# Reordering the loads that open each layer of a two-layer decoder step

## What is computed

```python
z = x @ w_in            # 1024 -> conv gates, q, six k/v parts, attention gates, two merge gates
u = ua * sigmoid(ug)                              # branch A: causal depthwise conv (31 taps),
conv_out = silu(layer_norm(conv(u_ext))) @ w_conv_out     # LayerNorm, swish, projection
pkc, pvc, pks, pvs = gather_pages(cache, page_table)      # branch B: paged past K/V of the samples
k_cmp = compress(kc_all, cmp_pe_k, cmp_w1_k, cmp_w2_k)    # blocks of 32 rows -> one row
o_cmp, p_cmp = cmp_attention(q, k_cmp, v_cmp, q_pos)
o_slc = slc_attention(q_rot, ks_all, vs_all, q_pos, select_blocks(p_cmp, q_pos, n))
o_win = win_attention(q_rot, kw, vw)
m = sigmoid(g_a) * conv_out + sigmoid(g_b) * (gated sum of the three @ w_attn_out)
x = layer_norm(ALPHA * x + m @ w_o)
x = layer_norm(ALPHA * x + (silu(x @ w_gate) * (x @ w_up)) @ w_down)
```

## Time and profile before

| | us |
|---|---|
| median of 3 runs | 1043.68 |
| lowest, highest | 1042.11, 1046.44 |
| the profiled execution, device time | 1041.28 |
| its span, first to last instruction | 1039.5 |
| PE busy in it | 979.4 (94%) |

### The profile page before, as it was taken

One profiled execution on the slowest core, in us unless ns is written; L12 is line 12 of the kernel. 1 busy time (PEld: TensorE's weight loads), 2 busy tenths in 40 slices (PEclk: granted clock), 3 DMA queues, 4 the chain that ended last, 5 costly groups with the idle time before them and its releaser, 6 DMA issues.

```text
span 1039.5 us, 23311 instructions
## 1 busy us (share of the span) xinstructions
PE 979.4 (94%) x7438; PEld 928.7 (89%) x7438; DVE 603.1 (58%) x1370; ACT 524.5 (50%) x966; POOL 753.9 (73%) x1081
## 2 busy tenths in 40 slices
PE   6999989989999999999979999889989999999996
PEld 6898878878989999999979978888889999999996
DVE  2969765476577555512447795745685765554125
ACT  3352574465566655533444436745555565555335
POOL 5877746434978888898848786544369788889985
PEclk9999999999999999999999999999999999999999
DMA  8875586621446654454256566675124344445542
GB/s 302 282 252 201 183 275 212 231 80 62 163 153 206 232 202 163 162 182 162 85 198 235 162 199 193 240 232 194 64 71 160 134 163 163 163 163 170 175 143 107
DMA packets 78917, 185.09 MB, mean 178 GB/s; under 512 B 9538, under 2 KB 42690, under 8 KB 78530
## 3 DMA queue, kind: packets, MB, share of 16 engines
q1 hardware_dynamic: 70290, 167.03, 47.9%
q10 hardware_dynamic: 8352, 15.59, 4.5%
q0 software_dynamic: 144, 0.89, 0.2%
HBM read 170.90 MB, written 12.57 MB: 177 GB/s over the span
## 4 chain that ended last, share of the span: by engine, by line
POOL 52%; issue 25%; PE 20%; DMA 1%; POOLq 1%; DVE 1%; ACT 1%; ACTq 0%; SPq 0%; DVEq 0%
POOL w_lo L620 46%; PE proj L691 4%; PE proj L693 4%; PE proj L692 4%; POOL hid L643 3%; POOL res L641 2%; PE proj L714 2%; PE proj L712 2%; PE proj L713 2%; DMA res<-xT_in 1%; POOLq L638 0%; POOLq L614 0%; POOL res L650 0%; DVE res L1572 0%; DVE sig_u L1639 0%
## 5 line engine op out<-in xcount | busy, mean ns | idle before, releaser
L620 POOL TENSOR_TENSOR w_lo<-wch,w_hi 128x256 fp32r<-128x256 f32 x940 | 686.4, 768 | 267.9 <-ACT w_hi L1100 267.5
L691 PE MATMUL proj<-x_hi,w_hi 128*128 128x290 f32 (+1 forms) x1248 | 381.6, 306 | 23.2 <-POOL w_lo L620 22.1
L693 PE MATMUL proj<-x_lo,w_hi 128*128 128x290 f32 (+1 forms) x1248 | 372.7, 299 | 0.0
L692 PE MATMUL proj<-x_hi,w_lo 128*128 128x290 f32 (+1 forms) x1248 | 371.7, 298 | 0.0
L1100 ACT ACTIVATE w_hi<-wch 128x1024 fp32r<-128x1024 f32 x235 | 247.7, 1055 | 155.5 <-PE proj L714 84.2
L691 PEld LDWEIGHTS proj<-x_hi,w_hi 128*128 128x128 f32 x1248 | 237.7, 190 | 30.3 <-POOL w_lo L620 13.7
L692 PEld LDWEIGHTS proj<-x_hi,w_lo 128*128 128x128 f32 x1248 | 238.1, 191 | 0.6
L693 PEld LDWEIGHTS proj<-x_lo,w_hi 128*128 128x128 f32 x1248 | 237.6, 190 | 0.0
L712 PE MATMUL proj<-hid_hi,w_hi 128*128 128x288 f32 x352 | 104.3, 296 | 0.0
L714 PE MATMUL proj<-hid_lo,w_hi 128*128 128x288 f32 x352 | 104.1, 296 | 0.0
L713 PE MATMUL proj<-hid_hi,w_lo 128*128 128x288 f32 x352 | 103.5, 294 | 0.0
(11 more groups left out here) (288 smaller groups left out, 1521.8 us busy)
## 6 DMA issues: line engine op xcount, KB each, us to landing
wch<-weights_in SPq DMA_DIRECT2D x235, 512.0 KB, 3.7
pg<-slc_pages_in SPq DMA_DIRECT2D x128, 128.0 KB, 2.3
pg<-cmp_pages_in SPq DMA_DIRECT2D x96, 128.0 KB, 2.9
wn<-win_in SPq DMA_DIRECT2D x16, 512.0 KB, 5.2
win_out<-wn ACTq DMA_DIRECT2D x4, 2048.0 KB, 9.1
pg<-cmp_pages_in ACTq DMA_DIRECT2D x32, 128.0 KB, 3.8
hid<-w_in SPq DMA_DIRECT2D x2, 1024.0 KB, 5.8
kv_out<-kv ACTq DMA_DIRECT2D x2, 864.0 KB, 3.5
```

Source lines behind the costliest of these rows:

```text
L620: last = nc.gpsimd.tensor_tensor(lo[:, cols], raw[:, cols], hi[:, cols].bitcast(F32), ALU.subtract)
L691: mm(ps, hi[:, kb], x[0][:, kb, 0:n], start=kb == 0, stop=False)
L692: mm(ps, lo[:, kb], x[0][:, kb, 0:n], start=False, stop=False)
L693: last = mm(ps, hi[:, kb], x[1][:, kb, 0:n], start=False, stop=kb == KD - 1)
```

## The change

Six edits:

1. The page table is fetched by ACT, as its first instruction, and no longer by SP.
2. In the first layer SP's wait for the table moves from ahead of chunk 3 to behind it. The pages of the lead move one chunk later in both layers (behind chunks 3 to 18, no longer 2 to 17).
3. In the second layer the wait for the end of the layer before and the load of `sm` move from behind chunk 2 to behind chunk 4.
4. `w1` and `w2` move from behind chunk 3 to behind chunk 8, in both layers.
5. GpSimd issues the constants after its first three subtractions, no longer as its first work.
6. `small_in` counts `sm` alone; a new counter `w1_in` counts `w1` and `w2`, and PE waits for it ahead of the first compression matmul.

```diff
-        small_in = Signal("small_in", 3, 16)
+        small_in = Signal("small_in", 1, 16)
+        w1_in = Signal("w1_in", 2, 16)
...
-                    if j == SLOTS - 1:
+                    if j == (SLOTS - 1 if first else SLOTS + 1):
                         wait_alone(*x_ready(layer, 0))
                         small_in.up(sp.dma_start(sm[:], small[bass.ds(layer, 1)].rearrange("a p n -> p (a n)")))
                         if first:
-                            sp.dma_start(table[:], page_table).then_inc(table_in, 16)
                             load_past(layer)
-                            sp.wait_ge(table_in, 16)
-                    if j == SLOTS:
-                        small_in.up(sp.dma_start(w1_sb, w1[bass.ds(layer, 1)].rearrange("a p b (c w) -> p (a b) c w", c=KD)))
-                        small_in.up(sp.dma_start(w2_sb[0:64], w2[bass.ds(layer, 1)].rearrange("a e c d -> e (a c) d")))
-                    if EARLY - 2 * PAGES <= j < EARLY:
-                        n = j - (EARLY - 2 * PAGES)
+                    if j == SLOTS and first:
+                        sp.wait_ge(table_in, 16)
+                    if j == 8:
+                        w1_in.up(sp.dma_start(w1_sb, w1[bass.ds(layer, 1)].rearrange("a p b (c w) -> p (a b) c w", c=KD)))
+                        w1_in.up(sp.dma_start(w2_sb[0:64], w2[bass.ds(layer, 1)].rearrange("a e c d -> e (a c) d")))
+                    n = j - (EARLY - 2 * PAGES) - 1
+                    if 0 <= n < 2 * PAGES:
...
-            pool.dma_start(cst[:], consts).then_inc(const_in, 16)
             pool.memset(u_p[:, :, 0:TAIL], 0.0)
...
             for n in range(PAIRS):
                 low_part(0, n)
+            pool.dma_start(cst[:], consts).then_inc(const_in, 16)
...
-                pool.wait_ge(*small_in(layer, 3))
+                pool.wait_ge(*small_in(layer, 1))
...
                 if c == 0 and sp_ == 0:
+                    pe.wait_ge(*w1_in(layer, 2))
                     pe.wait_ge(*xc_ready(layer, 1))
...
+            act.dma_start(table[:], page_table).then_inc(table_in, 16)
             now = {}
...
-                dve.wait_ge(*small_in(layer, 3))
+                dve.wait_ge(*small_in(layer, 1))
```

More of the change, by code:

```diff
@@ L473, in _ @@
         def _(sp):
-            for sig in chunk_in + [small_in]:
+            for sig in chunk_in + [small_in, w1_in]:
                 sig.begin(sp)
```

## The result

The changed kernel takes **1034.27 us**, median of 5 runs (1034.04 to 1037.84), against 1043.68 before. The ratio is 0.9917, 95% interval [0.9899, 0.9936]: about 9 us faster, 7 to 11 with the interval. The span of its profiled execution is 1032.4 us.

The account below looks back on a forecast made before the run. PE bounds the kernel (94% busy), so time could come only from its waits: four waits of 7.27 us, less 0.1 for ACT's new first instruction, take 7.2 off the median 1043.68, giving 1036.5 us, range 1033 to 1041.5.

Parts of the forecast that it names:

- The four waits: PE's waits ahead of chunks 3 and 4 in both layers close: 2.67 us in the first, 4.60 in the second.
- The span: Whole profiled execution: forecast to be 1034.1 us with a span of 1032.3, after 7.2 us off.
- the drops of the clock: PE at its lower clock after some idle stretches: 1.7 us each, booked as spread unrelated to the loads.
- ACT's new first instruction: Start of the first layer: ACT's issue of the table fetch delays rounding by 0.1 us, at worst 1.3.
- Chunk 3 at about 9: First layer: SP issues chunk 3 at about 9.0, 6.3 us earlier, with 2.0 us to spare; chunk 4 has 1.1.
- no stretch as empty as 13 to 15 us: Sign in the opening: the transfer engines' dry stretch, 44 GB/s between 13 and 15 us, does not stay empty.
- Chunk 5 behind the constants: First layer: constants issued in the same moment as chunk 5 cost nothing, at worst 1.2 us given back.
- Rival A: Constants and w1 displace chunks PE awaits (1.2, 0.8 us), or ACT's issue costs 1.3: 1038 to 1040, chance 0.20.
- Rival B: Table as late from ACT as before; chunk 5 then costs at most 1 us: 1037.5, chance 0.05.
- The new waits: SP's wait for the table, PE's for w1, VectorE's and GpSimd's for sm, and later pages: all cost nothing.
- no wait of PE for GpSimd between 521 and 590: Sign at the change of layers: PE never waits there for GpSimd in the trace after.
- The closed gaps: Sign against the forecast: they return as longer PE waits for VectorE and ACT between 90 and 300 us.

Follow-up runs that it names:

- e1: Kernel before with only the change of layers reordered as in the changed kernel, opening left as before, split counter kept: 1040.61 us, ratio 0.9959.
- e2: Kernel before with only the first layer's opening reordered as in the changed kernel, change of layers left as before, split counter kept: 1039.66 us, ratio 0.9956.
- before_again: The kernel before, unchanged, run and profiled a second time: 1044.69 us (one run).
- e5: Changed kernel with GpSimd issuing the constants as its first work again: 1035.29 us, ratio 0.9911.
- e8: Changed kernel with two more loads of the constants' size (1.74 MB) right behind the constants: 1037.57 us (one run).
- e7: Changed kernel with the page table fetched by SP as before, its wait staying behind chunk 3: 1035.42 us, ratio 0.991.
- e4: The changed kernel, unchanged, run and profiled a second time: 1036.2 us, ratio 0.9919.
- e3: Changed kernel with ACT issuing the page table's fetch behind its rounding of chunk 0: 1034.83 us, ratio 0.9915.
- e10: e9 with output 0 starting when a quarter of chunk 0 is ready and SP loading the constants behind chunk 10: 1033.97 us, ratio 0.9904.
- e6: Changed kernel with w1 and w2 early again, behind chunk 3 in layer 1 and behind chunk 4 and sm in layer 2: 1038.94 us, ratio 0.993.
- e9: Changed kernel with VectorE reading output 5 ahead of eight taps, and ACT fetching the table behind its rounding of chunk 0: 1035.62 us, ratio 0.9919.

## Why the prediction was right

The prediction was 1036.5 us, within 1033.0 to 1041.5, faster by over 0.5%. Measured: 1034.27. By its own steps:

- **The four waits, 7.27 us.** Right, in places and in mechanism: none is left, e1 and e2 bring back two each, and before_again has all four. The two leads shortened by 3.8 and 4.6 us, against 2.67 and 4.60 forecast.
- **The span, forecast as 1032.3 and measured as 1032.4.** That it agrees to 0.1 us is partly luck. The first lead gained 1.1 us more than forecast, the first matmul came 0.5 later and *rest* was 0.7 longer. The clock was also on the side of the trace before: 0.991 over that execution, 0.989 over the one after.
- **A wait costs more than its figure.** With output 0 read at the same moment (16.52 before, 16.51 after), outputs 4 and 6 are read 3.2 us sooner, not 2.67. The view counts the idle time from a matmul's modelled end, 0.29 us behind its start, but the next one would have started 0.13 us behind it; and the first two matmuls behind a wait start 0.23 and not 0.13 us apart. By these starts each of the two waits costs some 0.26 us more than its figure. The sum took the figures as they stood.
- **Output 0.** The remaining 0.5 of the 3.8 us lies here. The first matmul came half a microsecond later (9.63), and the matmuls of output 0 ran slowly for 3.63 us and before for 4.84, so that the later start was absorbed. That is this pair of traces and not the change: e5 has 4.84 and e2 4.77 with chunk 3 just as early.
- **The clock.** The medians differ by 9.4 us and the two profiled executions by 7.1. I had booked the drops of the clock as spread that has nothing to do with the loads. But two of three traces of the old opening have one behind a wait, and the clock over whole executions is lower in the kernel before (0.9873 against 0.9894, some 2 us by estimate): a closed wait is also a drop that can't follow it. That this is the whole of the difference isn't shown.
- **ACT's new first instruction, 0.1 us.** Its place in the chain was right. It delays ACT's table load by 0.4 us, of which chunk 0's landing hides all or a part. The first matmul, forecast at 9.2, came at 9.63, short of the 10 that would have spoken against the prediction.
- **Chunk 3 at about 9, 2.0 us to spare; no stretch as empty as 13 to 15 us.** 9.53; subtracted at 20.8 and wanted at 22.85; and 131 GB/s: right. Chunk 4 had 2.4 us to spare and not 1.1, as it was done at 17.96 + 5.70 = 23.66.
- **Chunk 5 behind the constants, at worst 1.2 us given back.** It was issued at 17.14 and rounded at 24.05, 6.9 us, between the 5.8 that I took from chunk 4 of before and the 8.7 with all of the constants on top. It was subtracted by 28.02 (25.19 + 2.83), wanted at 29.3. Chunk 6 was closer still: subtracted by 31.6, wanted at 32.4. Rival A stayed away by this 0.8 us; e8 shows it arriving.
- **Rival B, a late table.** e7 comes near it, with the first pages at 12.84, though not as late as the 14.39 of before. It costs nothing that can be seen, and not 1 us.
- **The new waits, "All nothing".** The sign itself, no wait of PE for GpSimd between 521 and 590, held in the changed kernel's two traces. But e4 has 1.37 us there for VectorE. What the step had missed is in "VectorE wants it after output 3, at 536": it looked at when VectorE's work may begin and not at how long its queue then is. The question "what is late next" had been asked of the loads alone. Its size, 0 to 1.4 us in these two, is inside the range.
- **The closed gaps "come back as longer waits between 90 and 300 us".** They don't; from the compression of one layer to the first matmul of the next the lengths are 429.8 us before and 430.5 after. But one wait in each layer, of PE for ACT's `sq`, is 2.1 to 4.3 us long in different traces of the same code, and the two of them together (4.7 to 7.7) are much of the spread of *rest*.

The likeliest time was 2.2 us too high. The ratio it stands for, 0.9931, is inside the measured interval, so the miss is no larger than the measurement can tell; the clock and the underpriced waits are its likeliest causes.

## What to carry to other kernels

When one queue issues loads in program order, look for a wait in it that belongs to none of the loads behind it, and put the loads whose slots are already free ahead of it. That is where the gain came from here. The place of the constants and the issuer of the table, each undone by itself, were worth nothing that could be measured; `w1`'s place stayed open. Compare stretches between fixed points of the program rather than the whole span, and price an idle wait of PE at its length, the restart and the chance of a clock drop behind it. After closing a wait, add up the queue of every engine that had used it to catch up.

## What the runs showed of the hardware

- **The clock's drop after a wait isn't a function of the wait's length.** 2.28, 2.79 and 3.05 us were followed by a drop, 1.99, 2.46 (e8) and 3.40 were not. The wait ahead of layer 2's first matmul, 1.64 to 2.21 us long in all thirteen traces, is followed by one in six of them (after, e1, e3, e5, e8, e10): 1.79 us of wait with a drop in e8, without in e6. The Trainium skill, TensorE: Matmul & The Clock Gate, "What's actually happening", says that the point at which the clock turns varies from run to run, and these traces agree.
- **The slow phase at the start varies.** Matmuls of 288 columns started 0.24 us apart for 3.01 us (e9), 3.63 (after), 4.84 (before, e5) and 4.94 (e10) from the first one on, then 0.13. The granted clock reads 1.00 in both phases, so it can be seen only from the matmuls.
- **Small VectorE operations cost over three times as much beside GpSimd.** The two lines L1788 and L1789 on 8 and 16 columns took 0.59 and 0.66 us in e4, while GpSimd subtracted without a break. In the opening of the changed kernel they fell into a gap of GpSimd from 28.02 to 28.78:

```profile
28.56 0.17 DVE L1788 TENSOR_SCALAR half_gb<-sm 128x8 f32<-128x8 f32 x1
28.76 0.18 DVE L1789 TENSOR_SCALAR alpha_gb<-sm 128x16 f32<-128x16 f32 x1
```

  The Trainium skill, SBUF — State Buffer, "SBUF: two separate sides", says that a GpSimd operation and a VectorE operation of certain kinds (one in a two-port mode, or one with two inputs in SBUF) lock a shared port pair against each other for a whole instruction. These times fit that: GpSimd's operation here takes 0.71 us (2.83 / 4), and VectorE's 0.17 becomes at most that. That these two operations ran in such a mode no trace shows.
- **The transfer rate has more room than the earlier trace rows showed.** 301 GB/s at a share of 0.95 looked full; 367 came in the changed kernel and 399 in e5 and e8, at shares of 1.01 to 1.03. So the share alone doesn't give the room; why the rates differ isn't shown.
